# Gathering the token rows of a mixture of experts for two pairs of experts at a time, in products of 256 columns, on one Trainium2 core

## The reference

```python
def moe_ffn(u, w_router, b_router, w1, w3, w2, ws1, ws3, ws2):
    xf = u.reshape(T, D)                          # T = 256 tokens, D = 1024
    ...                                           # idx, w: the 8 chosen of 64 experts of each token, and their weights
    def expert_block(args):
        toks, e, wts = args
        out = swiglu(xpad[toks], w1[e], w3[e], w2[e])     # FF = 256
        return out * wts[:, None].astype(out.dtype)
    y = lax.map(expert_block, (slot_tok, block_e, slot_w))
    routed = jax.ops.segment_sum(y.reshape(n_slots, D), slot_tok, num_segments=T + 1)[:T]
    shared = swiglu(xf, ws1, ws3, ws2)
    return (routed + shared).reshape(B, S, D)
```

## Time and profile before

| what | value |
|---|---|
| three runs | 2112.2, 2111.25, 2114.88 us (median 2112.2) |
| the profiled execution | 2107.32 us, span 2105.6 us |
| TensorE busy | 2028.0 us, 96% |
| VectorE busy | 1020.2 us, 48% |
| ScalarE busy | 392.8 us, 19% |
| mean DMA rate over the span | 284 GB/s |
| expert loop of the first layer | 389.45 us to about 903 us |
| expert loop of the second layer | 1263.11 us to about 1778 us |
| pairs | 66: 33 in each layer, 17 first pairs and 16 second ones |

### The profile page before, as it was taken

The page is one execution under the profiler, slowest core; times in us unless marked ns, Lnnn a source line. Parts: engine busy times, 40 slices in busy tenths (PEclk is TensorE's granted clock), DMA queues, the critical chain, the costliest instruction groups (busy, mean ns, idle before and its releaser), DMA issues. The chain is left out here.

```text
span 2105.6 us, 30285 instructions
## 1 busy us (share of the span) xinstructions
PE 2028.0 (96%) x11316; PEld 1204.3 (57%) x11316; DVE 1020.2 (48%) x2031; ACT 392.8 (19%) x797; POOL 68.6 (3%) x145
## 2 busy tenths in 40 slices
PE   5999999899999999989999989999999997999998
PEld 3847884445455455466588654544545543475475
DVE  2897534444444444459774254444444443253252
ACT  2133211111111111123231011111111111132131
POOL 1000004000000000000000030000000000110000
PEclk9999999999999999999999989999999999999999
DMA  9654549799999999766455548999999997532621
GB/s 348 214 206 164 200 148 351 285 421 403 402 413 400 397 404 401 315 251 209 160 213 187 208 172 329 404 410 399 401 402 405 405 398 250 186 97 64 221 81 40
DMA packets 148133, 598.08 MB, mean 284 GB/s; under 512 B 13036, under 2 KB 17760, under 8 KB 96608
## 3 DMA queue, kind: packets, MB, share of 16 engines
q1 hardware_dynamic: 146656, 594.06, 73.1%
q0 software_dynamic: 1408, 3.10, 0.6%
HBM read 596.07 MB, written 1.05 MB: 284 GB/s over the span
## 5 line engine op out<-in xcount | busy, mean ns | idle before, releaser
L1257 PE MATMUL banks<-weight_ring,h_t 128*64 128x512 f32 x2112 | 464.6, 592 | 3.3 <-DVE h_t L2019 3.3
L1257 PEld LDWEIGHTS banks<-weight_ring,h_t 128*64 128x64 f32 x2112 | 152.9, 137 | 302.7 <-issue 300.9
L1245 PEld LDWEIGHTS banks<-z,sp_ 128*128 128x128 bf16 x3168 | 178.7, 98 | 58.7 <-issue 51.9
L1245 PE MATMUL banks<-z,sp_ 128*128 128x128 bf16 x3168 | 190.0, 220 | 5.1 <-DVEq L2009 5.1
L2024 DVE TENSOR_TENSOR z<-banks,z 128x256 f32<-128x256 f32 x66 | 28.0, 425 | 343.6 <-ACT z L1538 343.6
L951 PE MATMUL banks<-h_t,weight_ring 128*128 128x256 f32 x768 | 170.1, 380 | 0.0
L951 PEld LDWEIGHTS banks<-h_t,weight_ring 128*128 128x128 f32 x768 | 145.3, 190 | 21.3 <-issue 1.6
L2283 PE MATMUL banks<-weight_ring,h_t 128*128 128x512 f32 (+2 forms) x384 | 135.3, 512 | 1.5 <-DMA weight_ring<-in_w_in 1.5
L1307 PE MATMUL banks<-o_parts,slot_of 128*128 128x512 f32 x512 | 133.8, 403 | 0.0
L1282 PE MATMUL banks<-slots,conv 128*64 128x512 f32 x544 | 124.2, 598 | 3.2 <-DVE slot_weight L2034 3.2
L891 PE MATMUL banks<-h_t,weight_ring 128*128 128x256 f32 x512 | 113.0, 383 | 4.3 <-DVEq L1599 4.3
(11 more groups left out here) (490 smaller groups left out, 2261.3 us busy)
## 6 DMA issues: line engine op xcount, KB each, us to landing
weight_ring<-in_w SPq DMA_DIRECT2D x264, 1024.0 KB, 10.3
weight_ring<-in_w_in SPq DMA_DIRECT2D x36, 2048.0 KB, 10.6
slots<-in_w SPq DMA_DIRECT2D x68, 1024.0 KB, 9.5
weight_ring<-in_w_mod SPq DMA_DIRECT2D x24, 2048.0 KB, 13.0
qk<-in_w SPq DMA_DIRECT2D x32, 1024.0 KB, 8.6
z<-in_w SPq DMA_DIRECT2D x32, 1024.0 KB, 10.6
weight_ring<-in_w_out SPq DMA_DIRECT2D x8, 2048.0 KB, 7.8
weight_ring<-in_w_in SPq DMA_DIRECT2D x10, 1024.0 KB, 12.5
```

The lines of the kernel that those rows point to most:

```text
L1245: mm = nc.tensor.matmul(x_banks[half][:, kk * P:(kk + 1) * P], xn_parts[:, t, c, half * KT // 2 + kk, :], pick_hot[:, i % PAIRS, t, :], st ...
L1257: mm = nc.tensor.matmul(h_bank[own, :], x_blk[:, i, k, own], w13(2 * i + b)[:, :, k, :], start=(k == 0), stop=(k == KT - 1), skip_group_ch ...
```

## The change

- *Gather of a turn.* The 0/1 matrix is now made for a whole turn (`turn_hot`, 256 slots). The gather goes in quarters of two k rows: 2 x 2 x 3 = 12 products of 256 columns. A pair gathers two quarters for the next turn: the first pair quarters 0 and 1, the second pair quarters 2 and 3.
- *A holding buffer.* When the first pair gathers, x of the second pair of this turn is still needed. So the x of quarters 0 and 1 that belongs to the second pair goes to `x_held`, and ScalarE moves it to its place after the second pair's first products (`move_held`). x now lies in `z`, and the w2 buffer that was in `z` lies in `h_t`.
- *Eviction.* `block_x` takes a quarter out by two `tensor_scalar` operations (multiply and add in one), each 128x256.
- *Slot rows by comparison.* The two bf16 transposes and ScalarE's copy of them are gone. A seventh column of `pair_weights` holds the token's number, so four small products once a turn (`turn_slots`, in the second pair) give weight and token of each slot of the next turn, and `slot_rows` on VectorE compares a row of token numbers with the slot's token. The identity in bf16 is gone from the constants and the row of token numbers has come.
- *The last turn.* Both its pairs are gathered, also where there is no second one.
- *Entry.* The one-hot of the first turn and the first gather no longer wait for the extra blocks' lists. Quarters 0 and 1 and the two column halves of the shared second product alternate. The table loads into registers come later: on TensorE in the first pair, on VectorE after the last quarter, and the two of the second layer at the layer's start.

The diff of TensorE's and ScalarE's part:

```diff
+        turn_hot = cut[0].bitcast(BF16).rearrange("p (t s) -> p t s", t=T)
+        sig_pair = cut[1]
+        act_pair = sig_h[:, 0, :]
+        x_units = z_flat[:, 0:PAIRS * KT * P + KT // 2 * P].rearrange("p (u s) -> p u s", s=P)
+        x_blk = z_flat[:, 0:PAIRS * KT * P].rearrange("p (i k s) -> p i k s", i=PAIRS, k=KT)
+        x_held = x_units[:, PAIRS * KT:, :]
...
-                    z_flat[:, 0:T * D].rearrange("p (f n) -> p f n", f=2)]
+                    K.h_t[:].rearrange("p k n -> p (k n)").rearrange("p (f n) -> p f n", f=2)]
...
-                shared_w2(1, slots2[:, 1])
...
-                pe.wait_ge(table_ready.sem, table_ready.at(l))
-                pe.wait_ge(parts_ready.sem, parts_ready.at(l))
-                last_turn, second, no_second, nth, pairs, uses = block_count(pe, l)
-                def gather(it, i, half):
-                    pe.wait_ge(hot_ready, pairs(it, i))
-                    for kk in range(KT // 2):
+                def gather(it, q):
+                    pe.wait_ge(hot_ready, uses(it, 0))
+                    for u in range(2):
...
                             for c in range(PARTS):
-                                mm = nc.tensor.matmul(x_banks[half][:, kk * P:(kk + 1) * P],
-                                                      xn_parts[:, t, c, half * KT // 2 + kk, :], pick_hot[:, i % PAIRS, t, :],
+                                mm = nc.tensor.matmul(x_banks[q % 2][:, u * PAIRS * P:(u + 1) * PAIRS * P],
+                                                      xn_parts[:, t, c, 2 * q + u, :], turn_hot[:, t, :],
                                                       start=(t == 0 and c == 0), stop=(t == T - 1 and c == PARTS - 1))
                     mm.then_inc(gather_done, 1)
+                def turn_slots():
+                    for i in range(PAIRS):
+                        for t in range(T):
+                            at_pair = at_slot_weight + i * 2 * (PARTS + 1)
+                            mm = nc.tensor.matmul(o_bank2[:, at_pair:at_pair + 2 * PARTS + 1], turn_hot[:, t, i * P:(i + 1) * P],
+                                                  pair_weights[:, i, t, 0:2 * PARTS + 1], start=(t == 0), stop=(t == T - 1),
+                                                  skip_group_check=True)
+                    mm.then_inc(slots_done, 1)
...
                     for k in range(KT):
+                        if i == 0 and k in (4, 6):
+                            pe.wait_ge(x_ready, quarter(it, k // 2))
...
+                    if i > 0 and not last:
+                        turn_slots()
...
+                    pe.wait_ge(slot_of_ready, pairs(it, i))
...
+                    if i == 0:
+                        pe.wait_ge(x_ready, quarter(it, 1))
+                    elif not first:
+                        pe.wait_ge(x_moved, moved(it))
                     pair_h(it, i)
                     if not last:
-                        gather(it, i + 1, 0)
-                    if not first:
+                        if i > 0:
+                            pe.wait_ge(x_ready, quarter(it + 1, 0))
+                        gather(it + 1, 2 * i)
+                    if i > 0 or not first:
                         pe.wait_ge(o_ready, nth(it, 2 * i - 1))
                     if not last:
-                        gather(it, i + 1, 1)
-                    pair_turn(it, i)
-                    if not first:
+                        gather(it + 1, 2 * i + 1)
+                    pair_turn(it, i, last)
+                    if first and i == 0:
+                        turns.extend(turn_count(pe, l))
+                    else:
                         pair_add(it, i - 1)
                     pe.wait_ge(turned_ready, pairs(it, i))
-                    pe.wait_ge(weight_ready, pairs(it, i))
                     if not last:
-                        pe.wait_ge(x_ready, nth(it, 2 * i + 3))
+                        pe.wait_ge(x_ready, quarter(it + 1, 2 * i + 1))
+                        if i > 0:
+                            pe.wait_ge(weight_ready, uses(it + 1, 0))
                     pair_w2(it, i)
-                for half in range(2):
-                    gather(0, 0, half)
+                pe.wait_ge(parts_ready.sem, parts_ready.at(l))
+                pe.wait_ge(sh_act_t_ready.sem, sh_act_t_ready.at(l, T))
+                gather(0, 0)
+                shared_w2(1, slots2[:, 1], (0,))
+                pe.wait_ge(table_ready.sem, table_ready.at(l))
+                gather(0, 1)
+                shared_w2(1, slots2[:, 1], (1,))
+                turn_slots()
+                for q in (2, 3):
+                    pe.wait_ge(x_ready, quarter(0, q - 2))
+                    gather(0, q)
+                pe.wait_ge(weight_ready, uses(0, 0))
+                turns = []
                 for i in range(PAIRS):
-                    pair(0, i, first=(i == 0))
+                    pair(0, i, first=True)
+                last_turn, second, no_second = turns
                 with pe.Fori(1, last_turn) as it:
                     for i in range(PAIRS):
                         pair(it, i)
                 pair(last_turn, 0, last=True)
                 with pe.If(no_second < 1):
-                    pe.wait_ge(o_ready, nth(last_turn, 1))
-                    for half in range(2):
-                        gather(last_turn, 1, half)
                     pair(last_turn, 1, last=True)
                 last_add()
...
+                def move_held(it):
+                    act.wait_ge(x_ready, quarter(it, 1))
+                    nc.scalar.activation(x_blk[:, 1, 0:KT // 2, :], x_held, ACT.Copy).then_inc(x_moved, 1)
...
+                    if i > 0 and not last:
+                        move_held(it + 1)
+                    copy_turned(it, i)
```

and of VectorE's:

```diff
+                def one_hot(it):
+                    col = ds(it * UNROLL, UNROLL)
+                    v.tensor_tensor(turn_hot.rearrange("p t (b s) -> p t b s", b=UNROLL), broadcast(place[:, :, 0, col], 3, SLOTS),
+                                    broadcast(broadcast(K.ramp[:, 1:1 + SLOTS], 1, UNROLL), 1, T), ALU.is_equal)
+                    for i in range(PAIRS):
+                        own = ds(it * UNROLL + 2 * i, 2)
+                        v.tensor_copy(pair_weights[:, i, :, 0:2 * PARTS].rearrange("p t (b c) -> p t b c", b=2),
+                                      weight_parts[:, :, own, :])
+                    dve.drain().then_inc(hot_ready, 1)
...
+                split_weights(slice(0, N_EXPERTS))
...
+                                        1.0 + t * P, None, ALU.add)
+                one_hot(0)
...
-                dve.wait_ge(table_ready.sem, table_ready.at(l))
-                dve.sem_inc(wait_carrier, 1)
-                last_turn, second, no_second, nth, pairs, uses = block_count(dve, l)
...
-                    dve.wait_ge(gather_done, nth(it, 2 * i + half))
-                    ks = slice(half * KT // 2, (half + 1) * KT // 2)
-                    x = x_blk[:, i % PAIRS, ks, :]
-                    v.tensor_tensor(x, x_banks[half][:].rearrange("p (k s) -> p k s", k=KT // 2), broadcast(mod_col[:, 3, ks], 2, P), ALU.mult)
-                    dve.drain()
-                    v.tensor_tensor(x, x, broadcast(mod_col[:, 2, ks], 2, P), ALU.add).then_inc(x_ready, 1)
+                split_weights(slice(N_EXPERTS, MAX_BLOCKS))
+                def block_x(it, q, held=False):
+                    dve.wait_ge(gather_done, quarter(it, q))
+                    for u in range(2):
+                        k = 2 * q + u
+                        out = x_units[:, k:k + 2 * KT + 1:2 * KT, :] if held else x_units[:, k:k + KT + 1:KT, :]
+                        last = v.tensor_scalar(out, x_banks[q % 2][:, u * PAIRS * P:(u + 1) * PAIRS * P].rearrange(
+                            "p (i s) -> p i s", i=PAIRS), mod_col[:, 3, k:k + 1], mod_col[:, 2, k:k + 1], ALU.mult, ALU.add)
+                    last.then_inc(x_ready, 1)
...
+                def slot_weights(it, first=False):
+                    if not first:
...
+                    dve.wait_ge(slots_done, uses(it, 0))
+                    for i in range(PAIRS):
+                        at_pair = at_slot_weight + i * 2 * (PARTS + 1)
+                        to = i if first else 2 * i
+                        v.tensor_copy(slot_token[:, i:i + 1], o_bank2[:, at_pair + 2 * PARTS:at_pair + 2 * PARTS + 1])
+                        for b in range(2):
+                            own = slice(b * SLOTS, (b + 1) * SLOTS)
+                            weights = v.tensor_reduce(slot_weight[own, to:to + 1],
+                                                      o_bank2[own, at_pair + b * PARTS:at_pair + (b + 1) * PARTS], AX.X, ALU.add)
+                    dve.drain().then_inc(weight_ready, 1)
+                def slot_rows(it, i, last=False):
+                    if last:
+                        v.tensor_scalar(slot_of[:, PAIRS], K.token_row[:], slot_token[:, i:i + 1], None, ALU.is_equal)
```

(22 more changed lines are left out.)

134 lines of the change are left out of this document (56 added, 78 removed).

## The result

The changed kernel takes 2090.1 us (median of 4 runs, 2087.8 to 2093.1), the kernel before 2111.7 beside it: a ratio of 0.9897, interval 0.9877 to 0.9916. It is 21.6 us faster. The prediction had 2100 us, 12.4 us faster, with 2093 as the lower end: the direction was right, the size was not.

What follows compares the result with a forecast made beforehand. TensorE was taken as the bound, DMA 0.5 us a pair behind. Two layers of 4.35 + 0.5 + 0.05 + 0.17 make 10.1, plus 2.3 for the loop starts: 12.4 us saved, 2100 us, range 2093 to 2109.

Steps and rivals of the forecast that it cites:

- The gather: TensorE's gather for a turn: 48 products of 256 columns at 109.3 ns, a pair's share 2.62 us, 0.07 less.
- rival E: Gather gets faster by instruction count, weight loads setting its pace: 2077 us; chance 0.02.
- Each pair loses two bf16 transposes and two products of 6 columns, 0.12 + 0.05 us.: TensorE's short slot-row work removed from every pair: 0.12 us for the transposes, 0.05 for the products.
- The slot products, 0.15: Four added products of 7 columns in each turn's second pair cost 0.10 to 0.22 us, taken as 0.15.
- I take a gain of 0.05 for the second pair: Second pair of a turn: VectorE and TensorE meet within 0.1 us, so 0.05 gained where TensorE alone gives 0.09.
- Rival C: Slower: the slot-weight wait before second pairs' second products becomes a bound; 2120 us at 0.64 a turn, 2137 at 1.2; chance 0.08.
- A turn: Two pairs in the loop save 0.24 + 0.05 = 0.29 us, over 15 turns in each layer 4.35.
- First pair's second products: After the entry they wait for the second quarter's eviction instead of weights: gain 0.5 us.
- last pair: The last pair of a layer's loop saves 0.17 us.
- The entries: Starts of the two layers' loops: first products 0.35 and 1.95 us earlier, 2.3 together.
- against the list products: Sign the forecast is right: first products 0.35 and 1.95 us earlier, measured from the list products.
- So I assume full clock: Second layer's entry: TensorE idles 2 us before the first gather, instead of 3.21, and then runs at full clock.

Runs made afterwards that it cites:

- e1: Changed kernel with two bf16 transposes of 128 columns put back behind the f32 ones in every pair; loop 5.28 us longer, 0.165 a pair.
- e2: As e1, with two products of 6 columns behind the bf16 transposes as well; median 2114 us, 2108 at clock 0.988.
- e9: Changed kernel with the gather in products of 128 columns, one pair's slots after the other's; loops 493.44 us.
- e5: Changed kernel with the slot products ahead of the last gather half; loop 1.19 us shorter in the first layer, 0.51 longer in the second.
- e6: Changed kernel with three extra VectorE copies ahead of the slot weights in every second pair; second pair 0.66 us longer in the first layer, 0.91 in the second.
- e7: Changed kernel with TensorE's old entry order, whole shared second product before the gather; list products to first products 10.23 us against 12.23 in the first layer.
- e10: Changed kernel with the edits of e7 and e5 together; median 2086.7 us, the changed kernel's beside it 2087.2.
- e12: As e10, with TensorE's two waits for the w2 loads moved ahead of the others; 2082.2 us, 0.9849 of the kernel before.
- e4: Kernel before without its two bf16 transposes of the slot rows in each pair, output not the reference's; a pair goes from 15.62 to 15.51 us.
- e13: As e6, with TensorE's two waits for the w2 loads moved ahead of its others; second layer's loop 502.05 us instead of 505.68.
- e3: Changed kernel with each gather product of 256 columns issued as two of 128 side by side on the same weights; loops 493.44 us.

## Why the prediction fell short

- **The bound.** Right: TensorE before and after, every turn the sum of its pieces, DMA below its pace.
- **The gather,** 109.3 ns a product forecast, 109.6 measured, 0.06 us a pair instead of 0.07. Right; rival E is out. The Trainium skill (TensorE: Matmul & The Clock Gate, Wait — 56ns, not 53.3ns?) gives columns over 2.4 GHz plus 2.5 ns, an estimate of 55.8 and 109.2 ns. By that rule the trace agrees at both widths (56.0 and 109.6 ns), and not with the pace that the same page gives for streams.
- **"Each pair loses two bf16 transposes and two products of 6 columns, 0.12 + 0.05 us."** This step failed. They were priced by their own starts, 0.17 in sum. e1 and e2 put them at 0.236: 0.08 more falls on the row ahead of them, by the load rows for the weight load that follows it. e9 adds another 0.05 in the first pair, where the transposes now stand behind a wide product. First pair: 0.06 + 0.05 + 0.165 + 0.07 = 0.35, and measured 15.62 - 15.27 = 0.35; the forecast had 0.24. The surplus is 0.11 in each first pair.
- **The slot products, 0.15.** They take 0.10 themselves and 0.08 on the transposes behind them (e5 shows it): 0.18, slightly under-priced.
- **"I take a gain of 0.05 for the second pair"**: measured 0.18. It is the first pair's 0.35 less 0.17 for the slot products. VectorE took nothing of it: its chain, forecast within 0.1 us of TensorE, ended 0.43 us ahead, since the evictions took 0.3 us less than priced and the small operations 0.2. But the warning was sound in the second layer: the release takes 0.25 us longer there, so only 0.07 is left (e6). Rival C needed a chain 0.64 us longer than forecast; it was shorter.
- **A turn:** 0.29 forecast, 0.53 measured. 15 turns in each of two layers times the missing 0.24 are 7.2 of the 9.2 us by which the forecast was short. The items below give about 1 us more. The rest is not explained; the way from the first loop to the second alone differs by 1.6 us between the three profiles of the changed kernel.
- **First pair's second products,** 0.5 forecast, 0.79 measured in the first layer (0.98 in the second); last pair 0.17 and 0.24.
- **The entries,** 0.35 and 1.95 forecast. By the starts it was 0.49 and 2.00, but in the first layer that is luck. The prediction took TensorE's arrival at 379.4 from an execution in which the shared product before it ran 1.7 us long at the lower clock, and so saw a wait of 0.5 us for the one-hot; at full clock it is 2.05. By its own sign, "against the list products", the first products come 0.93 us later there, not 0.35 earlier. In the second layer the 2.00 from the cast holds, and it is mostly the clock, which the prediction had seen. The prediction did not ask what the interleaving on TensorE was for, and e7 shows that it costs 2.0 us in the first layer and 0.45 to 2.2 in the second.
- **"So I assume full clock"** at the second layer's entry held in the changed kernel's own three profiles, and not always: in e5, whose entry is the same code, the clock fell to 0.50 behind a wait of 2.17 us, and the way from the list products took 14.07 us instead of 12.39.
- The waits inside the first products cost nothing (6.97 us as before), ScalarE's copies nothing, as forecast.

## What to carry to other kernels

A short product on TensorE is not priced by its own row: the row ahead of it grows too, and more so behind a narrow product, so price it by the stretch between the two long products around it, and put it between wide ones. When an early operand opens a hole, fill the hole with work that stands ready, instead of cutting that work in pieces around it. Put the wait that ends last at the end of the list of waits: two waits behind it cost 0.2 us a turn where it was the bound (e6), and 0.1 where it was only just so (e10 against e12), in the layer whose counts are worked out in registers. And before a start time is compared between two executions, check that the stretch ahead of it ran at the same clock in both.

## What the runs showed of the hardware

- Two f32 transposes of 128 columns take 0.16 us between a 256-column bf16 product and an f32 one, 0.21 behind a 128-column one, 0.24 with a short bf16 product either behind or ahead of them, 0.30 with a 128-column product ahead and a short bf16 one behind, and 0.32 with short ones on both sides (the changed kernel, e9, e1, e4, and e1's second pair).
- From the end of VectorE's last operation to TensorE's first product: 0.13 us in the first layer, 0.38 in the second, and 0.18 there (0.17 in the first layer) once no further waits stand behind (e6, e13).
- The DMA engines moved 421 to 423 GB/s over whole pairs, where the stretch in the earlier trace rows showed 416.
- Repeating the weights for two successive 128-column products gained nothing (e3 and e9: 493.44 us both).
- The total of the kernel before goes with the mean granted clock, 1.45 us for each thousandth, and three series of the changed kernel with the same loops have medians 3 us apart.
- Behind an idle of 3.2 us of TensorE in the second layer the gather of before ran partly at the lower clock in both profiles that have it (4.48 us, and 4.11 in e4, instead of 2.85). Behind 2.0 to 2.2 us the next products were at full clock in the changed kernel (1.47 us for a quarter), and in e5 they fell behind 2.17 (the shared half 3.35 us instead of 1.88).
